# A transformer block's first gate vector: twelve summing steps instead of eight inside the QKV groups, and another order of its loads

## What is computed

```python
mod_lat = (silu_c @ ada_w[i] + ada_b[i])[:, None, :]
sh1, sc1, g1, sh2, sc2, g2 = jnp.split(mod_lat, N_MOD, axis=-1)
h_lat = modulate(rms_norm(x, norm_mix_g[i]), sh1, sc1)
q_l, k_l, v_l = project_qkv(h_lat, attn_w_qkv[j], attn_q_norm_g[j], attn_k_norm_g[j])
k_c, v_c = project_kv(h_ctx, attn_w_qkv[j][:, D_MODEL:], attn_k_norm_g[j])
o_lat = latent_attention(q_l, k_l, v_l, k_c, v_c) @ attn_w_o[j]
x = x + g1 * o_lat
```

## Time and profile before

| | us |
|---|---|
| median of 3 runs | 2008.24 |
| lowest, highest | 2007.26, 2008.89 |
| the profiled execution | 2007.61 |
| its span, first to last instruction | 2005.8 |
| TensorE busy in it | 1967.7 (98%) |
| VectorE busy in it | 1386.6 (69%) |
| ScalarE busy in it | 969.4 (48%) |

### The profile page before, as it was taken

One profiled execution on the slowest core, in us unless ns is written; L12 is line 12 of the kernel. 1 busy time (PEld: TensorE's weight loads), 2 busy tenths in 40 slices (PEclk: granted clock), 3 DMA queues, 4 the chain that ended last, 5 costly groups with the idle time before them and its releaser, 6 DMA issues.

```text
span 2005.8 us, 25016 instructions
## 1 busy us (share of the span) xinstructions
PE 1967.7 (98%) x10204; PEld 1609.2 (80%) x10204; DVE 1386.6 (69%) x1420; ACT 969.4 (48%) x1265; POOL 111.1 (6%) x196
## 2 busy tenths in 40 slices
PE   6999999999999999999999999999999999999998
PEld 4677756778888888888888788788888888888886
DVE  3666898879868787788878775766666455555456
ACT  6432565445544445544444454555554454444444
POOL 1111001100000000000000000000000000000000
PEclk9999999999999999999999999999999999999999
DMA  9998768769989899799999726577776566555653
GB/s 358 338 379 315 278 257 295 287 237 324 358 288 353 314 363 354 271 363 365 357 354 359 273 85 190 175 249 253 257 250 223 185 196 210 189 192 196 221 189 126
DMA packets 152261, 542.80 MB, mean 271 GB/s; under 512 B 9393, under 2 KB 10577, under 8 KB 114641
## 3 DMA queue, kind: packets, MB, share of 16 engines
q1 hardware_dynamic: 119312, 335.77, 47.7%
q0 software_dynamic: 31744, 201.34, 27.2%
q10 hardware_dynamic: 1090, 4.09, 0.5%
HBM read 535.91 MB, written 2.10 MB: 268 GB/s over the span
## 4 chain that ended last, share of the span: by engine, by line
PE 92%; DVE 3%; DMA 2%; ACT 1%; issue 1%; POOL 0%; ACTq 0%; DVEq 0%; POOLq 0%
PE ps L2098 13%; PE ps L2032 11%; PE ps L2036 11%; PE ps L2035 11%; PE ps L2096 11%; PE ps L2099 6%; PE ps L1848 6%; PE ps L2095 6%; PE ps L1849 5%; PE ps L1850 5%; PE ps L2257 1%; PE ps L2204 1%; PE ps L1913 1%; DMA spare<-in_ada_w 1%; PE ps L2242 1%
## 5 line engine op out<-in xcount | busy, mean ns | idle before, releaser
L1201 DVE TENSOR_TENSOR w_lo<-raw,w_hi 128x1024 fp32r<-128x1024 f32 x616 | 749.3, 1223 | 472.2 <-ACT w_hi L727 472.0
L727 ACT ACTIVATE w_hi<-raw 128x1024 fp32r<-128x1024 f32 x616 | 649.2, 1059 | 848.1 <-PE ps L2036 345.8
L2098 PE MATMUL ps<-hh,w_hi 128*128 128x512 f32 x1088 | 426.9, 398 | 1.7 <-DVE hh L1627 1.7
L2032 PE MATMUL ps<-w_hi,hh 128*128 128x512 f32 x992 | 386.1, 389 | 1.5 <-DVE w_lo L1201 1.5
L2035 PE MATMUL ps<-w_lo,hh 128*128 128x512 f32 x992 | 386.0, 389 | 0.0
L2036 PE MATMUL ps<-w_hi,hh 128*128 128x512 f32 x992 | 385.9, 389 | 0.0
L2096 PE MATMUL ps<-hh,w_hi 128*128 128x512 f32 x960 | 379.9, 396 | 0.0
L2099 PE MATMUL ps<-hh,w_lo 128*128 128x256 f32 x1088 | 302.8, 278 | 0.0
L2095 PE MATMUL ps<-hh,w_lo 128*128 128x256 f32 x960 | 267.5, 279 | 0.0
L2099 PEld LDWEIGHTS ps<-hh,w_lo 128*128 128x128 f32 x1088 | 205.3, 189 | 40.8
L2032 PEld LDWEIGHTS ps<-w_hi,hh 128*128 128x128 f32 x992 | 186.2, 188 | 40.5 <-DVE w_lo L1201 1.9
(11 more groups left out here) (252 smaller groups left out, 1618.4 us busy)
## 6 DMA issues: line engine op xcount, KB each, us to landing
raw<-in_mlp_w SPq DMA_DIRECT2D x256, 1024.0 KB, 5.4
ada_raw<-in_ada_w POOLq DMA_DIRECT2D x151, 1024.0 KB, 6.0
spare<-in_ada_w POOLq DMA_DIRECT2D x29, 1024.0 KB, 7.0
raw<-in_attn_w_qkv SPq DMA_DIRECT2D x24, 1024.0 KB, 10.4
raw<-in_attn_w_o SPq DMA_DIRECT2D x16, 1024.0 KB, 7.7
raw<-in_fourier_w_o SPq DMA_DIRECT2D x16, 1024.0 KB, 5.1
g_row<-in_ada_w POOLq DMA_DIRECT2D x12, 1024.0 KB, 9.0
g_row<-gate_rows SPq DMA_DIRECT2D x48, 64.0 KB, 5.2
```

What stands on the lines that cost most here:

```text
L727: act.activation(w_slot(s)[0], raw[:, piece % RAW, s % 2, :], ACT.Copy).then_inc(hi_ready, 1)
L1201: nc.vector.tensor_tensor(lo, raw[:, s // 2 % RAW, s % 2, :], hi.bitcast(F32), ALU.subtract).then_inc(lo_ready, 1)
L2032: ins = mm(bank_of(tt, nb), h_hi[:, k % KT, tok], hi[:, cols], start=start, stop=False)
L2098: mm(both, w_hi[:, s % SPLIT, w], hh[:, k, :, :], start=(k == 0), stop=False, skip_group_check=True)
```

## The change

Steps 0 to 11 of the sum now stand in the second and third group, ahead of the adding of products 4, 6, 8, 10, 12 and 14 (`GATE_AT`); steps 12 to 14 take the places in the fourth group that 8 to 10 had, and step 15 the one at attention's first step. Attention's other four steps are gone. V0 to V11 use the two alternating buffers. On GpSimd's queue one V load now follows each S load from S19 on, but for S24 and S30, and the list behind S31 is shorter by the four loads that moved, with V15 behind V21.

```diff
+GATE_AT = (4, 6, 8, 10, 12, 14)
...
-    if i < 8:
+    if i < 12:
         return (7, 3)[i % 2]
...
-            elif i == 8:
+            elif i == 12:
                 pool.wait_ge(ada_mm, 32)
-            elif i == 9:
+            elif i == 13:
                 pool.wait_ge(ada_mm, 30)
             elif i < 16:
                 pool.wait_ge(ada_used, i - 1)
...
             elif i == 18:
-                pool.wait_ge(ada_used, 7)
+                pool.wait_ge(ada_used, 11)
...
-        for a in range(6):
-            load_start(19 + 2 * a)
-            load_start(20 + 2 * a)
-            load_vector(2 + a)
+        for a in range(12):
+            load_start(19 + a)
+            if a % 6 != 5:
+                load_vector(2 + a - a // 6)
         load_start(31)
-        for i in (8, 9, 16, 17, 10, 11, 18, 12, 19, 20, 21, 13, 14, 22, 23, 15):
+        for i in (12, 13, 16, 17, 18, 14, 19, 20, 21, 15, 22, 23):
             load_vector(i)
...
             if p >= 18:
-                for t in ((8, 9), (10,), (), ())[p - 18]:
+                for t in ((12, 13), (14,), (), ())[p - 18]:
                     ada_step(0, t)
             for r in range(products_before(p), products_before(p + 1)):
-                if g in (1, 2) and r % 16 in (4, 7, 10, 13):
-                    ada_step(0, 4 * (g - 1) + (r % 16 - 4) // 3)
+                if g in (1, 2) and r % 16 in GATE_AT:
+                    ada_step(0, 6 * (g - 1) + GATE_AT.index(r % 16))
...
             if n == 0:
-                ada_step(0, 11)
+                ada_step(0, 15)
...
-            if n in (1, 3, 6, 10):
-                ada_step(0, 12 + (1, 3, 6, 10).index(n))
```

## The result

| | us |
|---|---|
| before, median of 4 runs (lowest, highest) | 2008.13 (2007.26, 2008.89) |
| after, median of 4 runs (lowest, highest) | 2064.89 (2063.51, 2067.59) |
| ratio after to before, 95% interval | 1.0288 (1.0275 to 1.03) |
| after, the profiled execution, and its span | 2063.51, 2061.7 |

The change makes the kernel 56.8 us slower. The forecast was 2058, with a range of 2040 to 2076: the sign and the range were right, the middle was 7 us too low.

A forecast was written before the change was run, and what follows sets the result against it. TensorE, busy 98% of the span, was taken as the bound, with GpSimd's queue order deciding: S-load waits 37.0, clock 8.5, attention 5.1, less 0.5, is +50.1 us on 2007.61, so 2058; range 2040 to 2076.

The follow-up runs named there:

- experiment 6: Changed kernel, two variants: each S load one V load earlier on GpSimd's queue, 2036.79 us; or S issued before V after the same step's wait, 2052.32 us.
- experiment 5: Changed kernel with extra TensorE matmuls that add zeros just ahead of six waits for S loads; 2058.71 us.
- experiment 3: Changed kernel with S loads queued where they are ready and V15 right behind V14; 2006.06 us, against 2007.92 for the kernel before beside it.

## What to carry to other kernels

On a queue that issues in order, a load must not stand behind one that waits for something later than it does: write down for each load when its own condition comes true, and sort by that. Moving work off one engine pays at a wait only if no other engine's list ends at the same time; read the releaser in the wait's row, then ask what each engine on both sides was doing in the last few microseconds. And a load that already arrives just in time over busy DMA engines isn't improved for free: one place earlier for S31 was one place later for V9, and cost more.

## What the runs showed of the hardware

- The landing time of the same 1 MB load went from 5.1 us to 14.4, with what else was under way: 5.1 to 5.5 alone or first of a pair, 7.2 to 7.4 second of a pair, 8.3 to 14.4 where weight loads, and in part other pairs, were under way beside it. The DMA engines' busy share alone doesn't tell the two apart: it was 1.01 during S27's 7.3 us in after and 1.04 during S21's 10.9, but the weight queue moved 0.71 MB in the one and 1.98 in the other. A chain over a landing can therefore get longer as the kernel around it gets faster (experiment 6), which an estimate made from the slow kernel misses.
- An idle time of 2.5 us was enough for TensorE's clock to fall to 1.2 GHz for 3.4 us, but not in every execution of the same kernel; in experiment 5 one of 1.8 us was enough. It is worth about 1.7 us each time that TensorE works throughout the stretch. The scatter of some 6 us between runs of one kernel goes with it: of the 27 executions beside experiment 3, the three with a mean clock of 0.998 took 2006.0 us on average, and the six with 0.996 took 2008.9.
